# First layer of a four-layer transformer: six modulation loads with buffers of their own, v's weight remainders on GpSimd, h's remainders one quarter later

## The reference, cut to what matters

```
c_act = jax.nn.silu(c)
mod = jnp.einsum('bd,dm->bm', c_act, w_mod[i]) + b_mod[i]
sh_a, sc_a, gt_a, sh_f, sc_f, gt_f = jnp.split(mod, N_MOD, axis=-1)
h = modulate(rmsnorm(x, g_mix_pre[i]), sh_a, sc_a)      # h * (1 + sc_a) + sh_a
qkv = jnp.einsum('bsd,de->bse', h, w_qkv[i])
```

## Time and profile before

| | us |
|---|---|
| median of 3 runs (lowest to highest) | 1442.07 (1440.08 to 1444.54) |
| the profiled execution | 1436.95 |
| its span, first to last instruction | 1435.7 |
| TensorE busy | 1324.8 (92% of the span) |
| VectorE busy | 1051.9 (73%) |
| ScalarE busy | 735.8 (51%) |
| GpSimd busy | 104.8 (7%) |
| granted TensorE clock, mean | 0.971 |

### The profile page before, as it was taken

How to read it: one execution, slowest core, us unless ns; L and a number is a source line. 1 busy time by engine, 2 the same in 40 slices (tenths; PEclk the granted TensorE clock), 3 DMA queues, 4 the chain that set the end, 5 groups by cost and what they waited for, 6 DMA issues and landing times.

```text
span 1435.7 us, 21937 instructions
## 1 busy us (share of the span) xinstructions
PE 1324.8 (92%) x8728; PEld 1187.1 (83%) x8728; DVE 1051.9 (73%) x1628; ACT 735.8 (51%) x1233; POOL 104.8 (7%) x146
## 2 busy tenths in 40 slices
PE   4899899999979899999767999789999899999999
PEld 3798799988777689997556767579998799899987
DVE  6777798887658687889746775778887688666643
ACT  3655755554836565543643554564444554644442
POOL 0022000000024000000023141200000000000000
PEclk9999999999999989999879999999999999999999
DMA  8865578789466436668611512338788566356651
GB/s 342 340 235 206 191 283 302 268 296 368 184 250 242 169 118 237 248 235 312 264 69 70 203 48 105 138 127 322 304 306 333 215 246 268 140 212 240 230 197 53
DMA packets 48038, 320.03 MB, mean 223 GB/s; under 512 B 5360, under 2 KB 8000, under 8 KB 10560
## 3 DMA queue, kind: packets, MB, share of 16 engines
q1 hardware_dynamic: 47936, 318.63, 58.9%
HBM read 317.51 MB, written 1.10 MB: 222 GB/s over the span
## 4 chain that ended last, share of the span: by engine, by line
PE 66%; DVE 17%; ACT 7%; issue 4%; DMA 4%; POOL 2%; SPq 1%; ACTq 0%; DVEq 0%; POOLq 0%
PE mat L582 13%; PE mat L583 12%; PE mat L584 12%; PE mat L620 7%; PE mat L622 7%; PE mat L624 7%; DVE wlo L1481 6%; DVE raw L1499 4%; ACT whi L1047 3%; PE mat L640 1%; POOL st L2069 1%; PE mat L939 1%; DMA raw<-in_qkv 1%; PE mat L941 1%; PE mat L940 1%
## 5 line engine op out<-in xcount | busy, mean ns | idle before, releaser
L1481 DVE TENSOR_TENSOR wlo<-raw,whi 128x1024 fp32r<-128x1024 f32 x393 | 476.4, 1227 | 182.5 <-ACT whi L1047 180.9
L582 PE MATMUL mat<-hHL,whi 128*128 128x256 f32 x1864 | 533.8, 286 | 2.7 <-DVE tmp L1984 1.4
L583 PE MATMUL mat<-hHL,whi 128*128 128x256 f32 x1864 | 529.6, 284 | 0.0
L584 PE MATMUL mat<-hHL,wlo 128*128 128x256 f32 x1864 | 529.4, 284 | 0.0
L1047 ACT ACTIVATE whi<-raw 128x1024 fp32r<-128x1024 f32 x393 | 406.5, 1052 | 214.4 <-DMA raw<-in_down 61.0
L582 PEld LDWEIGHTS mat<-hHL,whi 128*128 128x128 f32 x1864 | 360.2, 193 | 9.1 <-issue 3.3
L583 PEld LDWEIGHTS mat<-hHL,whi 128*128 128x128 f32 x1864 | 360.3, 193 | 0.1
L584 PEld LDWEIGHTS mat<-hHL,wlo 128*128 128x128 f32 x1864 | 360.0, 193 | 0.0
L1499 DVE SCALAR_TENSOR_TENSOR raw<-raw,cB 128x1024 f32<-128x1024 f32 x192 | 234.1, 1228 | 8.7 <-DMA raw<-in_mod 8.7
L620 PE MATMUL mat<-whi,aHL 128*128 128x512 f32 x352 | 113.2, 391 | 1.7 <-DVE wlo L1481 1.7
L622 PE MATMUL mat<-wlo,aHL 128*128 128x512 f32 x352 | 112.3, 389 | 0.0
(11 more groups left out here) (207 smaller groups left out, 1508.1 us busy)
## 6 DMA issues: line engine op xcount, KB each, us to landing
raw<-in_mod SPq DMA_DIRECT2D x96, 1024.0 KB, 6.1
raw<-in_qkv SPq DMA_DIRECT2D x48, 1024.0 KB, 6.9
raw<-in_gate SPq DMA_DIRECT2D x44, 1024.0 KB, 4.9
raw<-in_up SPq DMA_DIRECT2D x44, 1024.0 KB, 5.2
raw<-in_down SPq DMA_DIRECT2D x44, 1024.0 KB, 5.3
raw<-in_wo SPq DMA_DIRECT2D x16, 1024.0 KB, 4.9
gtb<-gates SPq DMA_DIRECT2D x8, 512.0 KB, 6.3
cB<-in_crow SPq DMA_DIRECT2D x3, 512.0 KB, 7.8
```

The source lines that it names most:

```text
L582: pe.matmul(o, wh[:, k, :], hH[:, k, :], start=(k == 0), stop=False)
L583: pe.matmul(o, wh[:, k, :], hL[:, k, :], start=False, stop=False)
L584: m = pe.matmul(o, wl[:, k, :], hH[:, k, :], start=False, stop=(k == KT - 1))
L1481: dve.tensor_tensor(out=wlo[:, n % NSPL, :], in0=raw[:, f % NRAW, 1024 * h:1024 * h + 1024], in1=whi[:, n % NSPL, :].bitcast(f32), op=ALU. ...
```

## The change

**Own places.** The six modulation tiles of quarters 1 to 3 leave `raw` and FETCHES and get six tiles of 128x2048 in a tensor `begin`, which lies where `aHL`, `att` and others are used later. SyncE issues a quarter's two right behind v's weight tile of the quarter ahead, with no wait of their own; each has its semaphore. With fewer entries in FETCHES, v's third and fourth weight tiles reuse places 0 and 1, which quarter 0's steps set free. The first tile of all is loaded in two halves, the first with a semaphore of its own. The loads of `cB` for the later rows move from behind v's fourth weight tile to behind the eighth tile of weights.

**GpSimd.** The pieces 0 to 7 of `wlo` are made by a GpSimd `tensor_tensor` of the same shape; VectorE begins at piece 8, ahead of which it waits for all eight.

**Order.** VectorE makes `hL` of quarter q after the first two steps of quarter q+1 (`start_low`), and scales x by its norm (`vector_start_scale`) after all four steps of quarter 0 instead of after two. ScalarE makes `whi` 0 and 1 first of all, then in each quarter `tmp`, `tmp`, `hH`, `hH` and the two pieces of `whi` of the next quarter.

The core of the diff:

```diff
+START_LOADS = {("w", q - 1): [("mod", 0, 1, q), ("mod", 0, 0, q)] for q in (1, 2, 3)}
+START_PLACE = {item: i for i, item in enumerate(sum(START_LOADS.values(), []))}
...
-        if item not in FETCH_OF:
+        if item not in FETCH_OF and item not in START_PLACE:
...
+        start_loads = [begin[:, 2048 * i:2048 * i + 2048] for i in (0, 1, 2, 4, 5, 6)]
...
+                if f == 0:
+                    sp.dma_start(raw[:, i, 0:1024], src[:, 0:1024]).then_inc(s_first, 16)
+                    sp.dma_start(raw[:, i, 1024:2048], src[:, 1024:2048]).then_inc(s_raw[i], 16)
...
+                for ahead in START_LOADS.get(item, []):
+                    place = START_PLACE[ahead]
+                    sp.dma_start(start_loads[place], A["mod0"][4 * ahead[2] + ahead[3]]).then_inc(s_start[place], 16)
...
+                if item == ("w", 7):
                     for c in (1, 2):
                         sp.dma_start(cB[:, c, :], A["crow"][c:c + 1, :].to_broadcast([P, D])).then_inc(s_cin[c], 16)
...
-            for k in range(KT):
-                y = start_rows(k)
-                if k % 2 == 0:
-                    act.wait_ge(s_mod, FIN_AT[0, 1, k // 2])
-                act.activation(y, start_tile(k), ACT.Identity, bias=modc[:, 0, k:k + 1], scale=modc[:, 1, k:k + 1]
-                               ).then_inc(s_tma, 1)
-                hi(1)
-                act.wait_ge(s_tma, k + 1)
-                act.activation(hH[:, k, :], y, ACT.Copy).then_inc(s_hh, 1)
+            for q in range(4):
+                act.wait_ge(s_mod, FIN_AT[0, 1, q])
+                for k in (2 * q, 2 * q + 1):
+                    act.activation(start_rows(k), start_tile(k), ACT.Identity, bias=modc[:, 0, k:k + 1],
+                                   scale=modc[:, 1, k:k + 1]).then_inc(s_tma, 1)
+                for k in (2 * q, 2 * q + 1):
+                    act.wait_ge(s_tma, k + 1)
+                    act.activation(hH[:, k, :], start_rows(k), ACT.Copy).then_inc(s_hh, 1)
+                if q < 3:
+                    hi(2)
...
-        done_lo = [0]
+
+        done_lo = [8]
...
+        def start_low(q):
+            for k in (2 * q, 2 * q + 1):
+                dve.wait_ge(s_hh, k + 1)
+                dve.tensor_tensor(out=hL[:, k, :], in0=start_rows(k), in1=hH[:, k, :].bitcast(f32), op=ALU.subtract
+                                  ).then_inc(s_hl, 1)
...
+                    if q and (p, j) == (1, 2 * q + 1):
+                        start_low(q - 1)
+                if q == 0:
+                    for t in range(2):
+                        vector_start_scale(t)
+                    dve.wait_ge(s_small, 16)
                 start_columns(q)
...
+            start_low(3)
+            dve.wait_ge(s_lo, 8)
...
+            for n in range(8):
+                c, half = CHUNK_OF[n]
+                pool.wait_ge(s_hi, n + 1)
+                pool.tensor_tensor(out=wlo[:, n % NSPL, :], in0=raw[:, FETCH_OF["w", c] % NRAW, 1024 * half:1024 * half + 1024],
+                                   in1=whi[:, n % NSPL, :].bitcast(f32), op=ALU.subtract).then_inc(s_lo, 1)
```

More of the change, by code:

```diff
@@ L223, in sem @@
             return stack.enter_context(nc.semaphore(name))
+        with nc.sbuf_tensor("begin", [P, 14336], f32) as begin:
+            pass
         with nc.sbuf_tensor("att", [P, 10240], f32) as att, nc.sbuf_tensor("oHL", [P, 2, KT, S], f32r) as oHL:
@@ L258, in build @@
         s_raw = [sem(f"s_raw{i}") for i in range(NRAW)]
+        s_first, s_start = sem("s_first"), [sem(f"s_start{i}") for i in range(len(START_PLACE))]
         s_small, s_x, s_tab, s_subln, s_ctx, s_out = (sem(n) for n in (
@@ L522, in sync_program @@
                     src = A[f"mod{l}"][4 * p + q]
-                sp.dma_start(raw[:, i, 0:src.shape[-1]], src).then_inc(s_raw[i], 16)
+                if f == 0:
+                    sp.dma_start(raw[:, i, 0:1024], src[:, 0:1024]).then_inc(s_first, 16)
+                    sp.dma_start(raw[:, i, 1024:2048], src[:, 1024:2048]).then_inc(s_raw[i], 16)
+                else:
+                    sp.dma_start(raw[:, i, 0:src.shape[-1]], src).then_inc(s_raw[i], 16)
+                for ahead in START_LOADS.get(item, []):
+                    place = START_PLACE[ahead]
+                    sp.dma_start(start_loads[place], A["mod0"][4 * ahead[2] + ahead[3]]).then_inc(s_start[place], 16)
                 if item in GATE_OUT:
@@ L1487, in mod_step @@
         def mod_step(l, p, j):
-            f = FETCH_OF["mod", l, p, j // 2]
-            src = raw[:, f % NRAW, 1024 * (j % 2):1024 * (j % 2) + 1024]
-            dve.wait_ge(s_raw[f % NRAW], 16 * (f // NRAW + 1))
+            item = ("mod", l, p, j // 2)
+            if item in START_PLACE:
+                tile = start_loads[START_PLACE[item]]
+                dve.wait_ge(s_start[START_PLACE[item]], 16)
+            else:
+                f = FETCH_OF[item]
+                tile = raw[:, f % NRAW, :]
+                if f == 0 and j == 0:
+                    dve.wait_ge(s_first, 16)
+                else:
+                    dve.wait_ge(s_raw[f % NRAW], 16 * (f // NRAW + 1))
+            src = tile[:, 1024 * (j % 2):1024 * (j % 2) + 1024]
             for c in rows_of(l, p):
@@ L1659, in vector_program @@
                     mod_step(0, p, j)
[L1660 to L1663, removed]
-                start_columns(q)
[L1665 to L1669, removed]
+                    if q and (p, j) == (1, 2 * q + 1):
[4 more added lines that the diff above has]
+                    dve.wait_ge(s_small, 16)
+                start_columns(q)
+            start_low(3)
+            dve.wait_ge(s_lo, 8)
             for l in range(LAYERS):
```

## The result

The changed kernel takes 1446.3 us (median of 18 runs, 1440.87 to 1450.27), and the kernel before 1441.97 us in the 18 runs beside it. The ratio is 1.0025 with a 95% interval of 1.0013 to 1.0037, so by the ratio the change costs 3.6 us, between 1.9 and 5.3 (the two medians lie 4.3 apart). That is within the 0.3% called no change ahead of the run, and inside the range. The forecast was +2.0 us.

What follows compares the result with a forecast made beforehand. VectorE was taken to bound the start; GpSimd's pieces and VectorE's work, added as one line, put q 1.6 or 3.3 us later, taken as +2.0: 1442.07 + 2.0 = 1444.1 us, range 1436.5 to 1449.5.

Steps and rivals of the forecast that it cites:

- What bounds the kernel: First 60 us: VectorE sets the pace, 9.9 us a quarter; no load stands in the chain after x.
- Loads: Start: loads issued without waits land second tile at 13.6 us, last modulation tile at 36.6, v's last weights at 39.2.
- The hold: Wlo pieces on GpSimd: VectorE and GpSimd exclude each other, each 128x1024 piece costing VectorE 2.14 us, ends 2.0 and 2.54.
- The sum: Both engines as one line: 17.4 us plus 34.5 gives last columns at 51.9, row 6 of v's product at 53.8.
- the two clocks: TensorE's rows 6 and 7: 5.5 us at full clock or 7.1 as before; q at 59.3 or 60.9, left open.
- The size: First q product 1.6 or 3.3 us later, taken as +2.0 us; the median then 1444.1 us.
- Overlap: Rival: GpSimd and VectorE overlap and loads bound; q 8.4 us earlier, about 1433.7 us; chance 0.15.
- Order of turns: Rival: GpSimd's last piece falls behind the last columns; q -0.5 to +1.1 us, about 1442.4; chance 0.16.
- Longer hold: Rival: 2.54 us per GpSimd piece between 17 and 52 us, with half clock; +6.4 us, about 1448.5; chance 0.20.
- What was queued behind: VectorE's pieces 8 and 9 follow at about 56 and 57 us; q's second half needs 9 at 62, 4 us room.

Runs made afterwards that it cites:

- experiment 4: The kernel before, with only own places and early issue for the six modulation loads; one run, 1437.66 us, first q product at 57.57 us.
- experiment 5: The kernel before, with only the new order on ScalarE and VectorE, loads and GpSimd as before; 1435.35 us against 1441.55, ratio 0.9957.
- experiments 6 and 9: Changed kernel with pieces back on VectorE, plus eight unused two-input GpSimd tensor_tensor instructions: 128x1024 in 6, 1452.42 us; 128x512 in 9, 1444.48 us.
- experiment 1: The changed kernel, with wlo pieces 0 to 7 back on VectorE; 1435.37 us against 1443.07 for the kernel before, ratio 0.9952.
- experiment 2: The kernel before, with only wlo pieces 0 to 7 moved to GpSimd, order and loads as before; one run, 1449.44 us.
- experiments 1 and 7: 7: changed kernel with pieces back on VectorE, plus eight unused GpSimd memsets of 128x1024; one run, 1439.29 us. 1 has its own line.

## Why the prediction was right

**What bounds the kernel.** Right, and shown: VectorE sets the pace and no load does. Loads alone changed nothing (experiment 4), and taking VectorE's waits away moved q by 7.9 us (experiment 5).

**Loads.** Right. The last of the six modulation tiles is issued at 10.4 us and the longest takes 25.9 us to land, so 36.3 against 36.6 forecast. VectorE's second tile came at 14.0 (13.6). SyncE's rows for the six:

```profile
L540 SPq DMA_DIRECT2D begin<-in_mod x6: 433/513/786, 4.8 to 10.4; - x6
...
DMA to landing us min/median/max: 14.2/20.9/25.9
```

**The hold.** Right. 2.14 us was taken for a 128x1024 piece, from one 128x512 place in the earlier trace rows, as twice 1.07. In the changed kernel the eight pieces lengthen the starts of the instructions beside them by 2.05 to 2.22 us, 17.3 in all (17.1 forecast), and experiments 6 and 9 (two inputs, 128x1024 and 128x512) give 2.15 and 1.05: a fixed part doesn't show. An estimate of 2.25 us came from the Trainium skill's GPSIMD Engine Reference (3.1); the 2.17 of the changed kernel (17.3 / 8) lies between it and the forecast.

**The sum.** One line for both engines: start 17.6 (17.4), last columns at 52.5 (51.9), row 6 at 54.45 (53.8), q at 60.02 (59.3 at full clock or 60.9 at half). The 0.6 us by which row 6 was later is 0.2 of start, 0.2 of holds, 0.1 of columns, and the rest small differences on the way. Of the two clocks it was the full one, which the prediction had left open. It named 1 to 3 us of idle time ahead of row 6; it was 0.64, since rows 4 and 5 had themselves run at half clock until 51.3 us and filled the gap. That step was not foreseen.

**The size.** +2.36 us at the first q product against +2.0, and +3.6 (1.9 to 5.3) by the ratio of the runs. That +2.0 came so close is in part luck: it was taken between +1.6 at full clock and +3.3 at half, and the case that came, full clock, was 0.7 us later than its own figure. The forecast lies at the low end of the measured interval. What an edit at the start gives came through to the end, within the intervals of the ratios: -7.9 us at q and -6.2 in all (interval -3.6 to -8.6) in experiment 5, -6.3 and -6.9 (-4.5 to -9.4) in experiment 1.

**The rivals.** *Overlap*: fell; the steps beside GpSimd take 3.4 us. Its one support was that the earlier trace rows are a single place, and the trace of the kernel before has more: at 777.71 us four pieces of `wlo` take 5.71 us beside a GpSimd instruction of 128x512, where four alone take 4.80. *Order of turns*: fell; GpSimd's eighth piece ends at 50.93, before the last step does. *Longer hold*: 2.54 was too much, 2.17 is the number. What none of the cases had was that the change is made of a gain and a larger loss. The order alone brings q 7.9 us forward (experiment 5), 1.6 of it by the clock. From there to the changed kernel q moves back by 10.2 us: eight pieces at 2.17 - 1.14 make 8.2, 1.4 is VectorE's wait ahead of its last `hL` rows, which its own two pieces would cover, and 0.5 is the second tile, at 14.00 instead of 13.48 us. The sum had both terms in it, as one line without VectorE's four waits of 1.6 us, but named only the result. Worked out for the kernel that leaves the pieces on VectorE, the same sum would have found the better version without a run: 8 x (2.14 - 1.14) = 8 us less, where experiment 1 is 8.7 us earlier at q.

**What was queued behind.** Right in its result: the later pieces on VectorE began at 55.20 and nobody waited for them before q.

## What to carry to other kernels

Here GpSimd was no second vector engine for work that reads SBUF. While it runs a two-input instruction, VectorE's own two-input instructions stand still (ones with a single input were not tried), and the profile calls that busy: compare durations of the same row with GpSimd idle and beside it, and add both engines' work as one line. Here a moved 128x1024 subtraction cost 2.17 us of VectorE's time against 1.14 for doing it there. A GpSimd instruction with one input cost 0.82, and VectorE's own one-input instruction of that size, the scaling of x, takes 0.67 from one start to the next. A wait that is repeated in every stage (here 1.6 us for `whi`) is worth more than an early load that nobody waits for, and it went by reordering alone.

## What the runs showed of the hardware that was not expected

The hold is not a property of VectorE's big instructions: in the changed kernel a VectorE instruction on 128x2 elements took 2.21 us instead of 0.16 (the row of 17.88 in the chain above).

A GpSimd instruction with one input holds VectorE for only a part of its own duration. It takes 2.8 to 3.6 us and costs VectorE 0.82:

```profile
45.97 2.05 DVE L1530 SCALAR_TENSOR_TENSOR begin<-begin,cB 128x1024 f32<-128x1024 f32 x1
...
45.04 3.63 POOL L2053 TENSOR_SCALAR tmp<-x 128x1024 f32<-128x1024 f32 x1 [0.16 <-POOL tmp L2053]
```

With two inputs the hold of 2.15 to 2.17 us is nearly the 2.4 us that a piece took in experiment 2. Why it is a part in the one case and nearly all in the other is open.

Issuing a load is not always cheap for SyncE. Before, the four small loads of the tables took it 0.43 to 0.47 us each, at 37 to 39 us. In the changed kernel they come at 17 us, behind some 9 MB of loads not yet landed (v's fourth weight tile, the last of them, lands at 38.8 us, and the loads run at some 420 GB/s), and three of them take 2.1 to 2.9 us, as they do to 0.1 us in experiments 1 and 7:

```profile
16.77 0.43 SPq L558 DMA_DIRECT2D att<-in_rope  x1
17.25 2.90 SPq L559 DMA_DIRECT2D att<-in_qkg  x1
20.19 2.13 SPq L560 DMA_DIRECT2D att<-in_lam  x1
22.36 2.13 SPq L561 DMA_DIRECT2D subln<-in_subln  x1
```

It cost nothing here, since nothing on SyncE's queue was urgent. Which limit it is (bytes, descriptors or entries) was not tried.
